# A hybrid diffusion step on one core: the second norm's first tile in halves, two modulation units moved ahead of the broadcast, and GpSimd's weight subtraction moved behind its other work

## The reference

```
h  = rmsnorm(x) * g1 * (1 + sc1) + sh1
q, k, v, bg, cg, xc = split(h @ w_in)
x += gate1 * (concat(attention, gated short convolution) @ w_out)
h2 = rmsnorm(x, norm2_g) * (1 + sc2) + sh2
a, b = split(dwconv3(h2 @ w_up))
x += gate2 * ((silu(a) * b) @ w_down)
```

## Time and profile before

| | us |
|---|---|
| median of three runs | 1589.41 (1584.88 to 1589.67) |
| profiled execution, time | 1589.34 |
| profiled execution, span | 1587.5 |
| TensorE busy | 1563.4 (98%) |
| VectorE busy | 1028.2 (65%) |
| ScalarE busy | 724.0 (46%) |
| GpSimd busy | 165.5 (10%) |
| mean granted clock | 0.991 |

### The profile page before, as it was taken

One profiled execution on the slowest core, in us unless ns is written; L12 is line 12 of the kernel. 1 busy time (PEld: TensorE's weight loads), 2 busy tenths in 40 slices (PEclk: granted clock), 3 DMA queues, 4 the chain that ended last, 5 costly groups with the idle time before them and its releaser, 6 DMA issues. The chain is left out here.

```text
span 1587.5 us, 26411 instructions
## 1 busy us (share of the span) xinstructions
PE 1563.4 (98%) x10573; PEld 1458.6 (92%) x10573; DVE 1028.2 (65%) x1661; ACT 724.0 (46%) x1218; POOL 165.5 (10%) x197
## 2 busy tenths in 40 slices
PE   8999999999999999999999999999999999999998
PEld 6678889988999999999987788899899999999998
DVE  6762666737775765757777547685687667476673
ACT  5434454326552643525444344542565355263452
POOL 1000000003211202112000000000221120120210
PEclk9999999999999999999999999999999999999999
DMA  9554010465756957769553621033377585694862
GB/s 360 201 191 152 28 54 28 160 210 156 179 146 158 215 137 170 184 153 209 155 175 109 207 71 54 27 107 108 93 161 178 142 196 150 153 207 137 193 156 84
DMA packets 284511, 236.13 MB, mean 149 GB/s; under 512 B 10698, under 2 KB 254724, under 8 KB 284388
## 3 DMA queue, kind: packets, MB, share of 16 engines
q1 hardware_dynamic: 260064, 189.89, 38.1%
q0 software_dynamic: 24080, 44.45, 16.2%
q10 hardware_dynamic: 244, 0.09, 0.0%
HBM read 188.78 MB, written 3.67 MB: 121 GB/s over the span
## 5 line engine op out<-in xcount | busy, mean ns | idle before, releaser
L1633 ACT ACTIVATE w_hi<-raw_all 128x1024 fp32r<-128x1024 f32 x120 | 126.2, 1056 | 234.1 <-DMA raw_all<-raw_all 113.4
L2230 DVE TENSOR_TENSOR w_lo<-raw_all,w_hi 128x1024 fp32r<-128x1024 f32 x120 | 146.6, 1222 | 115.3 <-ACT w_hi L1633 114.9
L1240 PE MATMUL ps<-gg,w_hi 128*128 128x322 f32 x704 | 218.5, 310 | 0.0
L1242 PE MATMUL ps<-gg,w_lo 128*128 128x322 f32 x704 | 218.2, 310 | 0.0
L1241 PE MATMUL ps<-gg,w_hi 128*128 128x322 f32 x704 | 218.1, 310 | 0.0
L666 POOL DMA_DIRECT2D raw_all<-raw_all x160 | 136.4, 868 | 620.6 <-DMA raw_all<-in_w_up_dram 493.9
L1185 PE MATMUL ps<-hc_lo,w_hi 128*128 128x322 f32 x640 | 199.5, 312 | 0.0
L1183 PE MATMUL ps<-hc_hi,w_hi 128*128 128x322 f32 x640 | 198.9, 311 | 0.0
L1187 PE MATMUL ps<-hc_hi,w_lo 128*128 128x322 f32 x640 | 198.6, 310 | 0.0
L1183 PE MATMUL ps<-ht_hi,w_hi 128*128 128x322 f32 x480 | 150.1, 313 | 5.6 <-ACT s L1651 5.2
L2125 DVE SCALAR_TENSOR_TENSOR x<-ps,modv,x 128x128 f32<-128x128 f32 (+2 forms) x240 | 90.4, 434 | 93.6 <-PE ps L1242 54.5
(11 more groups left out here) (235 smaller groups left out, 3488.9 us busy)
## 6 DMA issues: line engine op xcount, KB each, us to landing
raw_all<-in_w_up_dram SPq DMA_DIRECT2D x280, 256.0 KB, 3.8
raw_all<-raw_all POOLq DMA_DIRECT2D x160, 256.0 KB, 4.0
raw_all<-in_w_in_dram SPq DMA_DIRECT2D x48, 512.0 KB, 5.1
raw_all<-in_w_mod_dram SPq DMA_DIRECT2D x48, 512.0 KB, 4.3
raw_all<-in_w_down_dram SPq DMA_DIRECT2D x16, 768.0 KB, 4.5
raw_all<-in_w_down_dram SPq DMA_DIRECT2D x16, 640.0 KB, 4.1
mod_q<-in_w_mod_dram SPq DMA_DIRECT2D x8, 1024.0 KB, 9.1
raw_all<-in_w_out_dram SPq DMA_DIRECT2D x16, 512.0 KB, 4.3
```

The costliest lines, as they stand in the source:

```text
L1240: mm(out, wh[:, k, :], gh, start=k == 0, stop=False)
L1242: ins = mm(out, wl[:, k, :], gh, start=False, stop=k == kf - 1)
L1633: A(whi_b[:, 2 * i:2 * (i + 1), :], src, ACT.Copy).then_inc(up_hi[i], 1)
L2230: V.tensor_tensor(wlo_b[:, pair, :], raw_b[:, pair, :] if i else first_pair(g), whi_b[:, pair, :].bitcast(F32), ALU.subtract).then_inc(up_ ...
```

## The change

On TensorE the first unit "t" goes between the two parts of the sums, the second directly behind them, both ahead of the broadcast. The first tile of the norm is done in two halves of 322 columns on VectorE and ScalarE: VectorE's first half starts once three of the five token tiles are broadcast. The first gate tile takes the columns' first half for both weight halves, waits, and takes the second. VectorE's loop now runs one tile ahead instead of two, and ScalarE's first tile has functions of its own. GpSimd does its six prompt parts first; the weight half follows and also waits until six tiles of the norm are finished.

```diff
@@ GpSimd
-                pool.wait_ge(hi_done[1], l * SPLIT_SLOT + (G_U + 1) // 2 + 1)
-                pool.wait_ge(diag_ready, 3 * NT * (l + 1))
-                nc.gpsimd.tensor_tensor(w_lo[:, 1, :], raw[:, 1, :], w_hi[:, 1, :].bitcast(F32), ALU.subtract
-                                        ).then_inc(split_full[1], 1)
                 for k in range(POOL_FULL, KT):
                     pool.wait_ge(xr_ready, KT * l + k + 1)
...
+                pool.wait_ge(hi_done[1], l * SPLIT_SLOT + (G_U + 1) // 2 + 1)
+                pool.wait_ge(h2_ready, KT * l + KT - 2)
+                nc.gpsimd.tensor_tensor(w_lo[:, 1, :], raw[:, 1, :], w_hi[:, 1, :].bitcast(F32), ALU.subtract
+                                        ).then_inc(split_full[1], 1)
                 first_sum(FIRST)
@@ TensorE
-                stat(l, 2)
-
-                mod_sum(l, GAP_A[l], 0, "t", None)
+                stat(l, 2, lambda: mod_sum(l, GAP_A[l], 0, "t", None))
+                mod_sum(l, GAP_A[l], 1, "t", None)
                 spread(l, 2)
-                mod_sum(l, GAP_A[l], 1, "t", None)
...
+                    for i in range(4):
+                        h, s = divmod(i, 2) if k == 0 else (i % 2, i // 2)
+                        if g == 0 and k == 0 and i == 2:
+                            pe.wait_ge(h2_ready, KT * l + 1)
...
-                    pe.wait_ge(h2_ready, KT * l + k + 1)
+                    if k:
+                        pe.wait_ge(h2_ready, KT * l + k + 1)
+                    else:
+                        pe.wait_ge(h2_half, l + 1)
@@ ScalarE
+                def first_half_tile():
+
+                    act.wait_ge(xr_half, l + 1)
+                    for c0, n, s in ((C_PROMPT, SEQ, 0), (C_SAMPLE, HALF - C_SAMPLE, 1)):
+                        ins = A(hfull[:, 0, c0:c0 + n], hfull[:, 0, c0:c0 + n], ACT.Identity,
+                                bias=modv[:, 3, 0, s:s + 1], scale=gain[:, 0, s:s + 1])
+                    ins.then_inc(hf_half, 1)
+                    act.wait_ge(hf_half, l + 1)
+                    A(hb_hi[:, 0, 0:HALF], hfull[:, 0, 0:HALF], ACT.Copy).then_inc(hh2_half, 1)
+
+                def second_half_tile():
+
+                    act.wait_ge(xr_ready, KT * l + 1)
+                    A(hfull[:, 0, HALF:C_SAMPLE + DEC], hfull[:, 0, HALF:C_SAMPLE + DEC], ACT.Identity,
+                      bias=modv[:, 3, 0, 1:2], scale=gain[:, 0, 1:2]).then_inc(hf_ready, 1)
+                    act.wait_ge(hf_ready, KT * l + 1)
+                    A(hb_hi[:, 0, HALF:T], hfull[:, 0, HALF:T], ACT.Copy).then_inc(hh2_ready, 1)
@@ VectorE
+                b0, b1 = B_RMS[2]
+                dve.wait_ge(rb_full, 3 * NT * l + 2 * NT + 3)
+                V.tensor_tensor(hfv[:, 0, 0, :], x[:, 0, 0:HALF], ps[:, b0, 0:HALF], ALU.mult).then_inc(xr_half, 1)
                 dve.wait_ge(rb_full, 3 * NT * l + 3 * NT)
-                b0, b1 = B_RMS[2]
-                for i in range(KT + 2):
+                V.tensor_tensor(hfv[:, 0, 1, :], x[:, 0, HALF:T], ps[:, b1, 0:HALF], ALU.mult).then_inc(xr_ready, 1)
...
+                for i in range(1, KT + 1):
...
-                    if i >= 2:
-                        k = i - 2
+                    if i == 1:
+                        first_low(0, hh2_half, h2_half)
+                        first_low(1, hh2_ready, h2_ready)
+                    else:
+                        k = i - 1
```

More of the change, by code:

```diff
@@ L374, in hybrid_step @@
         modx_full, modt_full = sem("modx_full"), sem("modt_full")
+        xr_half, hf_half, hh2_half, h2_half = (sem(s) for s in ("xr_half", "hf_half", "hh2_half", "h2_half"))
         hf_ready, hp_ready, tap0_ready = sem("hf_ready"), sem("hp_ready"), sem("tap0_ready")
@@ L1152, in gate_tile @@
                     wh, wl = (half[:, g, :].rearrange("p (s t n) -> p s t n", s=2, n=P) for half in (w_hi, w_lo))
[L1153 to L1159, removed]
+                    for i in range(4):
+                        h, s = divmod(i, 2) if k == 0 else (i % 2, i // 2)
+                        if g == 0 and k == 0 and i == 2:
+                            pe.wait_ge(h2_ready, KT * l + 1)
+                        out = ps[:, B_GATE[g][s][h], 0:HALF]
+                        hh, hl = (half[:, k % KH, (B21 if k >= KH else B11) + h, :] for half in (hc_hi, hc_lo))
+                        mm(out, wh[:, s, k, :], hh, start=k == 0, stop=False)
+                        mm(out, wh[:, s, k, :], hl, start=False, stop=False)
+                        ins = mm(out, wl[:, s, k, :], hh, start=False, stop=k == KT - 1)
                     return ins
@@ L1544, in h_high @@
                     A(hb_hi[:, k % KH, base:base + T], hfull[:, k, :], ACT.Copy).then_inc(hh2_ready, 1)
-                for k in range(KT):
+                def first_half_tile():
[12 more added lines that the diff above has]
+                    A(hb_hi[:, 0, HALF:T], hfull[:, 0, HALF:T], ACT.Copy).then_inc(hh2_ready, 1)
+                first_half_tile()
+                second_half_tile()
+                for k in range(1, KT):
                     h_full(k)
@@ L2158, in _, with first_low @@
                 reciprocals(2)
+                b0, b1 = B_RMS[2]
+                dve.wait_ge(rb_full, 3 * NT * l + 2 * NT + 3)
+                V.tensor_tensor(hfv[:, 0, 0, :], x[:, 0, 0:HALF], ps[:, b0, 0:HALF], ALU.mult).then_inc(xr_half, 1)
                 dve.wait_ge(rb_full, 3 * NT * l + 3 * NT)
-                b0, b1 = B_RMS[2]
-                for i in range(KT + 2):
+                V.tensor_tensor(hfv[:, 0, 1, :], x[:, 0, HALF:T], ps[:, b1, 0:HALF], ALU.mult).then_inc(xr_ready, 1)
+                def first_low(h, read, ready):
+                    dve.wait_ge(read, (KT * l if h else l) + 1)
+                    cols = slice(h * HALF, (h + 1) * HALF)
+                    V.tensor_tensor(hb_lo[:, 0, cols], hfull[:, 0, cols], hb_hi[:, 0, cols].bitcast(F32), ALU.subtract
+                                    ).then_inc(ready, 1)
+                for i in range(1, KT + 1):
                     if i < KT:
```

## The result

| | before | after |
|---|---|---|
| median, us (7 runs each) | 1589.41 (1584.68 to 1592.61) | 1599.2 (1594.81 to 1602.18) |
| profiled execution / span, us | 1589.34 / 1587.5 | 1599.77 / 1597.9 |

The ratio is 1.0061, 95% interval 1.0043 to 1.0078. I had forecast 1592.0 in a range of 1585 to 1596 and given slower by over 0.3% a chance of 0.18. On the profiled executions the change costs 10.4 us where I had +2.6.

What follows compares the result with a forecast made beforehand. TensorE, busy 98% of the span, bound the kernel, at half clock in layer 0's second norm. 1589.34 plus 1.9 (layer 0 +1.2, layer 1 +0.7) plus 0.7 for clock falls gave 1592 us, range 1585 to 1596.

Steps and rivals of the forecast that it cites:

- The unit between the sums: TensorE, second norm: one modulation unit between the two sums costs +0.6 us in layer 0, 0 in layer 1.
- Full clock: Second unit ahead of the broadcast: clock stays full, TensorE free at t 3.5 (us from broadcast start), not 7.37.
- my case with a fall: Second norm: if the clock falls despite the new order, TensorE is free at t 6.4.
- rival C: Second norm: clock falls anyway, so the half tile starts nothing earlier; +3.1 us in all, 1593; chance 12%.
- The half tile: Norm's first tile in halves: TensorE starts gate products at t 3.6, then waits 1.3 us ahead of tile 1.
- The hold: End of first gate sweep: GpSimd's weight half shuts VectorE out of low half 7; sweep ends at t 23.2.
- Rival A: End of first gate sweep: GpSimd and VectorE don't hold each other up for long; 1585.8 us; chance 25%.
- rival B: End of first gate sweep: low half 6 is shut out too, sweep ends at t 24.9; 1597.6 us; chance 8%.
- Steps 1 to 4: Second norm through first gate sweep: layer 0 +1.2 us, layer 1 +0.7, clock falls +0.7 besides.
- step 5: Work queued behind the weight half: VectorE's combinations, SyncE's w_up blocks, GpSimd's sums, ScalarE's first weight copy; cost 0.
- Cost 0, with 2 us to spare.: Second gate sweep: copy at 393.5, ScalarE arrives at 401, sweep ends at 403.8, so late blocks cost nothing.
- Rival D: Behind the weight half: GpSimd's first sums land late; +3 us on top of the forecast, 1595; chance 5%.

Runs made afterwards that it cites:

- the experiment with only a hold: Kernel before plus an unused 2048-column GpSimd subtraction behind its parts and six tiles, awaited by VectorE's first combination: 1591.86 us, ratio 1.0020.
- only late blocks: Kernel before, with SyncE's first w_up block of each layer also waiting for the end of the first gate sweep: 1602.03 us, ratio 1.0071.
- four blocks first: Changed kernel, with SyncE issuing w_up blocks 8, 0, 2 and 3 ahead of its wait for the weight half: 1596.35 us, ratio 1.0042.
- behind all eight: Changed kernel, with GpSimd's weight half waiting for all eight finished tiles instead of six: 1602.95 us, ratio 1.0087.
- the first kernel in pieces: Changed kernel, weight half in four 512-column pieces ahead of the parts: two behind the diagonal, one behind each first-tile half: 1588.6 us, ratio 0.9992.

## Why the prediction was wrong, step by step

1. **The unit between the sums** cost +0.65 in layer 0 (second sums at 363.66, 363.01 before) and nothing in layer 1: as forecast, +0.6 and 0.
2. **Full clock** held in layer 1 (broadcast 1.60) and failed in layer 0: 0.50 from 364.9 to 368.2, broadcast 2.28, started 1.16 us later than before instead of 0.6. The clock was back at 368.2, so that TensorE was free at t 4.1, where my case with a fall had 6.4. This is the condition of rival C, and the order alone shows it too (2.18). I had read one stretch at 1.00, the first norm of layer 1, as what the order does; it shows what the order can do (how often, below).
3. **The half tile** started TensorE at t 4.5 and 3.8 (3.6 forecast) and the wait ahead of tile 1 was 1.04 and 1.05 (1.3). Right in layer 1, 0.9 late in layer 0 with the clock.
4. **The hold** was the likeliest case and came as worked out. Low half 7 took 4.47 us beside the weight half's 5.21, from t 17.2 to 21.7; TensorE waited 2.25 and 2.28 where I had 2.7, and tile 7 began at t 21.7 and 21.05 against 21.4. Rival A falls by this row and by the experiment with only a hold (4.38 us for a low part), rival B by the low half 6 of 0.83 us at 382.47 (the row ahead of the held one), but only just: low half 6 started 0.05 us ahead of the weight half in both layers, and in layer 1 of the kernel with only the weight half moved, where they started together, B's case came. That B stayed away in the change was luck more than working: I had put the two starts within 0.5 us of each other. The Trainium skill (SBUF — State Buffer, Who interferes with whom) says that whichever starts first keeps the pair for its whole instruction; these rows agree, now in both directions. Behind the stall the clock fell in layer 0 (0.50 at 389.5 to 391), which I had priced at 1.5 and given one chance in four; in layer 1 it did not (1.00 at 1157.8 to 1159.8). Steps 1 to 4 together: layer 0 +3.7 (1.2 from the later broadcast, 0.9 from tile 7, 1.6 from the clock) against +1.2 and a share of the clock, layer 1 +0.4 against +0.7 (the other 0.4 of its +0.8 is ScalarE's lateness, step 5).
5. **The step that failed: "Cost 0, with 2 us to spare."** I had the first sum issued near 389.5 and landing 3.5 later, the copy at 393.5, ScalarE free at 401. The issue came at 392.05, because low half 6, begun 0.05 us earlier, kept the weight half waiting (5.21 in place of 4.54) and the norm itself ran late, so that SyncE began 1.1 later than I had, and the two blocks of the first sum took 4.3 us to be there where I had 2.8; and the sum landed after 6.5 us, not 3.5. I took 3.5 from a row in which the DMA engines were 0.41 busy; here the remaining blocks of the same nine were in flight, at a share of 1.04. The copy came at 398.51, 5 us behind my 393.5. The 7 us of ScalarE's work behind it were right (7.0 with only late blocks), so they now end at 405.7, no longer at 401. In layer 0 that left 0.66 us ahead of the sweep's result, and only because the sweep too ended 3.7 later; in layer 1 ScalarE came 0.4 late. Behind it everything ScalarE hands over comes later: the waits for it grew by 2.0 us in layer 0 and 1.6 in layer 1, where besides the clock fell behind the wait of 2.87 and TensorE's busy time behind the sweeps grew from 62.5 to 63.7. That makes the +1.9 and +2.6 of the stretches. The Trainium skill (DMA: Bandwidth & Descriptors, Issuing engines are not separate DMA queues) states that transfers started by different engines run on the same 16 DMA engines and interleave; the windows fit it (3.5 and 6.5 us for the same 256 KB).

Rival D was this mechanism, and I had its condition ("sums land 3 us later") but gave it 5% and put it "up to 3 us a layer" at +3 in all. It measured +4.9 over the two layers, 0.4 of it ahead of the copy of layer 1. With +3.7 and +0.4 from the norms, that makes 9.0 of the 10.4 us; the 1.4 elsewhere is within the spread of the rest of the span. What stays open is why lateness is never made up: no run here separates the wait that the first group's late copy hands on from that of the next group's loads. They were shown only as one.

## What to carry to other kernels

When a step is moved behind others, cost the whole chain that is queued behind it, and take the duration of each transfer from a row in which the same other transfers are in flight; a margin of 2 us that rests on a quiet queue is none. An instruction that holds VectorE off can do so for its own length wherever VectorE next wants two SBUF inputs, be it for 8 columns; so look for that next step at the new place. Cut into pieces near its old place, the subtraction cost nothing here, but the change then gained nothing clear over the kernel before either. An engine released sooner gains nothing if the next in line isn't ready: the order alone put 2.05 and 2.80 us of waiting where slow work had been.

## What the runs showed of the hardware

- Where two subtractions of VectorE and GpSimd met, the one that started first ran at its usual length: low half 6 started 0.05 us ahead of the weight half, took its usual 0.83, and the weight half 5.21 in place of 4.53 to 4.60; where both are recorded at 1149.50, GpSimd's ran (4.57) and the low half took 5.25. Low half 7, which came 1.4 us behind the weight half's start, took 4.47 in place of 0.83. A low part that came 0.9 us behind the dummy subtraction took 4.38, and that one 4.59. The length of the held step doesn't matter: a sum over 8 columns took 4.56 in place of 0.17. And a GpSimd part of 0.45 that started during one low half took 1.62 and ended behind the next, which followed at once.
- The new order of TensorE does not decide the clock. Over the profiled executions of the six kernels that have it in both layers and of layer 1 of the two that have it there, the broadcast ran at half clock, in part or whole, 5 times of 14: in layer 0 of the change, of the order alone, of four blocks first and of behind all eight (2.18 to 2.42 us), and in layer 1 of the first kernel in pieces (2.48). It took 1.60 in the same layers of other kernels with the same instructions. I have no row that tells the two apart beforehand. The order does shift the odds: with the old one the broadcast of the second norm took 2.46 to 2.93 in all 10 cases. In the first norm of layer 1, which has the new order in every kernel, it took 1.60 in nine profiled executions and 2.67 to 2.93 in three.
- An accumulating transfer of 256 KB within SBUF took 3.5 to 3.6 us from its issue to GpSimd's next with the DMA engines 0.41 to 0.43 busy, and 4.5 to 7.3 with them 0.70 to 1.11 busy beside loads from HBM.
